# Gathered expert rows through SBUF as whole rows, and four of eight y sums held in PSUM

## What is computed

```
act = gelu(einsum('thkd,td->thk', u[idx], hb))
y   = einsum('thkd,thk->td', v[idx], g * act)      # written here with its operands swapped
x   = x + gate2 * y
```

## Time and profile before

| | |
|---|---|
| median of 3 runs | 3081.89 us (3079.91 to 3082.31) |
| span of the profiled execution | 3916.6 us, 45477 instructions |
| mean granted clock of TensorE in it | 0.894 of 2.4 GHz |
| busy: PE, DVE, POOL, ACT | 3146.4, 2357.3, 1734.0, 1532.9 us |
| first and last gelu of the expert part | 2193.17 and 3870.01 us |

### The profile page before, as it was taken

How to read it: one execution, slowest core, us unless ns; L and a number is a source line. 1 busy time by engine, 2 the same in 40 slices (tenths; PEclk the granted TensorE clock), 3 DMA queues, 4 the chain that set the end, 5 groups by cost and what they waited for, 6 DMA issues and landing times.

```text
span 3916.6 us, 45477 instructions
## 1 busy us (share of the span) xinstructions
PE 3146.4 (80%) x13344; PEld 2447.2 (62%) x13344; DVE 2357.3 (60%) x5010; ACT 1532.9 (39%) x2186; POOL 1734.0 (44%) x1714
## 2 busy tenths in 40 slices
PE   6998899894946749568385888888988998888896
PEld 3787567682735627446264666676766776666765
DVE  4624555451633526446351477787887887877788
ACT  2200543220211202112021356666665666666664
POOL 1002351215245263451523456666665665665663
PEclk8999799996967869678697999999999999999998
DMA  6514412231211212112132577777777777777776
GB/s 214 178 44 175 157 48 76 96 116 47 93 59 57 79 45 91 51 65 88 41 113 81 209 246 255 261 261 266 253 265 253 268 267 255 255 259 256 253 259 236
DMA packets 243601, 645.51 MB, mean 165 GB/s; under 512 B 54688, under 2 KB 55984, under 8 KB 242352
## 3 DMA queue, kind: packets, MB, share of 16 engines
q1 hardware_dynamic: 135856, 371.12, 26.4%
q0 software_dynamic: 107648, 273.25, 20.8%
HBM read 568.46 MB, written 75.76 MB: 164 GB/s over the span
## 4 chain that ended last, share of the span: by engine, by line
PE 30%; issue 17%; DVE 15%; another core or an unknown queue 14%; ACT 4%; DVEq 1%; ACTq 0%; DMA 0%; SPq 0%
PE ra_dots L1548 10%; DVE total L2245 6%; PE ra_dots L1552 5%; PE ex_y L2121 4%; PE ro_q_ps L1746 3%; PE ex_dots L2111 3%; DVE total L2214 2%; ACT ex_vhi L2181 2%; DVE px_ulo L1598 1%; PE ro_q_ps L1751 1%; PE ex_dots L2114 1%; DVE ex_wlo L2202 1%; DVE ex_vlo L2202 1%; ACT ex_prod L2162 1%
## 5 line engine op out<-in xcount | busy, mean ns | idle before, releaser
L2162 ACT ACTIVATE ex_prod<-ex_ring,ex_present 128x512 f32<-128x512 f32 x1024 | 692.6, 685 | 528.3 <-DVE total L2245 389.2
L2081 POOL DMA_INDIRECT ex_ring<-peer_v_dram,sp_row x512 | 534.0, 1043 | 503.7 <-ACT ex_prod L2162 375.1
L1718 POOL DMA_INDIRECT gate_scratch<-ro_dense_gate,ro_dense_place x512 | 502.0, 981 | 448.6 <-DVE ro_dense_gate L1875 293.6
L2245 DVE TENSOR_TENSOR total<-total,ex_prod 128x512 f32<-128x512 f32 x1016 | 670.8, 682 | 22.2 <-issue 13.4
L2076 POOL DMA_INDIRECT ex_pick<-act_scratch,sp_place x512 | 497.8, 972 | 244.2 <-issue 157.4
L1548 PE MATMUL ra_dots<-h_hi_a,px_uhi 128*128 128x512 f32 x1024 | 420.5, 411 | 210.1 <-ACT px_uhi L1530 116.9
L1537 DVE SCALAR_TENSOR_TENSOR px_ulo<-px_uhi,px_u 128x512 fp32r<-128x512 f32 x256 | 170.4, 708 | 606.4 <-ACT px_uhi L1530 493.1
L1560 ACT ACTIVATE ra_act<-ra_dots 128x512 f32<-128x512 f32 x128 | 76.7, 599 | 1007.4 <-remote 532.1
L1548 PE MATMUL ra_dots<-h_lo_a,px_uhi 128*128 128x512 f32 x1024 | 416.1, 406 | 57.0 <-issue 57.0
L2121 PE MATMUL ex_y<-ex_vhi,ex_whi 128*128 128x512 f32 x768 | 322.0, 419 | 160.2 <-DVE total L2214 131.9
L1552 PE MATMUL ra_dots<-h_hi_a,px_ulo 128*128 128x512 f32 x1024 | 285.9, 409 | 162.9 <-issue 143.1
(11 more groups left out here) (293 smaller groups left out, 5492.1 us busy)
## 6 DMA issues: line engine op xcount, KB each, us to landing
px_u<-peer_u_dram SPq DMA_DIRECT2D x256, 512.0 KB
px_v<-peer_v_dram SPq DMA_DIRECT2D x128, 512.0 KB
gate_scratch<-clear_zeros SPq DMA_DIRECT2D x16, 2048.0 KB, 18.7
act_scratch<-ra_act SPq DMA_DIRECT2D x128, 256.0 KB
ex_g<-gate_scratch SPq DMA_DIRECT2D x128, 256.0 KB
w_in_raw<-w_ada_dram SPq DMA_DIRECT2D x64, 256.0 KB, 3.5
w_ada_half<-w_ada_dram SPq DMA_DIRECT2D x4, 2048.0 KB, 13.9
ro_raw<-w_peer_q_dram SPq DMA_DIRECT2D x8, 1024.0 KB, 4.9
```

Of the source, the lines that this page charges most:

```text
L1718: nc.gpsimd.indirect_dma_start(elements, bass.IndirectOffsetOnAxis(ap=places[:, i:i + 1], axis=0), dense_gate[:, t, q:q + 1], None).then_i ...
L2081: nc.gpsimd.indirect_dma_start(ring[:, i], None, rows, bass.IndirectOffsetOnAxis(ap=which[:, RING * s + i:RING * s + i + 1], axis=0)).then ...
L2162: nc.scalar.activation(prod[:, h], ring[:, i, h * HALF:(h + 1) * HALF], ACT.Copy, scale=present[:, b, i:i + 1]).then_inc(prod_ready, 1)
L2245: nc.vector.tensor_tensor(total[:, t, at], total[:, t, at], prod[:, h], ALU.add).then_inc(row_added, 1)
```

## The change

`prod` moves from two PSUM banks of half rows to two SBUF buffers of whole rows. ACT's multiply and DVE's addition of the gathered rows then take 1024 elements at a time, 8 of each in a stage. The two banks go to `held`, so 4 of the 8 y blocks stay in PSUM over all stages, and 4 are added by DVE. In each half stage PE makes one y block, then the two held blocks, then the other y block; the stage orders of ACT and DVE are written anew for the smaller counts.

```diff
-    HELD = NY // 4
+    HELD = NY // 2
     ADDED = NY - HELD
+    HALF_STEP = ADDED // 2
...
+        prod = sb("ex_prod", [P, 2, D])
         dots = ps("ex_dots", [P, 2, TBD])
         held = ps("ex_held", [P, HELD, HALF])
         y = ps("ex_y", [P, 2, HALF])
-        prod = ps("ex_prod", [P, 2, HALF])
...
                         if s + 1 < ST:
-                            pool.wait_ge(prod_ready, 2 * (RING * s + i + 1))
+                            pool.wait_ge(prod_ready, RING * s + i + 1)
                             row(s + 1, i)
...
-                    for n in range(3 * part, 3 * part + 3):
-                        if n == 3 * part + 2:
-                            product(held[:, part], b, part, opens, closes).then_inc(held_ready, 1)
-                            pe.wait_ge(y_added, ADDED * s + n - 1)
-                        elif not opens or n >= 2:
+                    for n in range(HALF_STEP * part, HALF_STEP * part + HALF_STEP):
+                        if n % HALF_STEP:
+                            for m in range(HALF_STEP * part, HALF_STEP * part + HALF_STEP):
+                                product(held[:, m], b, m, opens, closes).then_inc(held_ready, 1)
+                        if not opens or n >= 2:
                             pe.wait_ge(y_added, ADDED * s + n - 1)
                         product(y[:, n % 2], b, HELD + n, True, True).then_inc(y_ready, 1)
...
-                def multiply(s, b, j, first):
-
-                    i, h = j // 2, j % 2
+                def multiply(s, b, i, first):
+
                     act.wait_ge(row_in[i], 16 * s + 16)
                     act.wait_ge(pick_weighted, s + 1)
-                    if not first or j >= 2:
-                        act.wait_ge(row_added, 2 * PER * s + j - 1)
-                    nc.scalar.activation(prod[:, h], ring[:, i, h * HALF:(h + 1) * HALF], ACT.Copy,
+                    if not first or i >= 2:
+                        act.wait_ge(row_added, PER * s + i - 1)
+                    nc.scalar.activation(prod[:, i % 2], ring[:, i], ACT.Copy,
                                          scale=present[:, b, i:i + 1]).then_inc(prod_ready, 1)
...
-                        dve.wait_ge(row_added, 2 * PER * s + j - 2 * NA + 1)
-                        nc.vector.tensor_tensor(total[:, t, at], total[:, t, at], prod[:, h], ALU.add).then_inc(row_added, 1)
+                        dve.wait_ge(row_added, PER * s + i - NA + 1)
+                        nc.vector.tensor_tensor(total[:, t], total[:, t], prod[:, i % 2], ALU.add).then_inc(row_added, 1)
...
                         weigh(s, c)
-                        sums(3 * c)
+                        sums(HALF_STEP * c)
                         rows(c, 0, 1)
                         if not last or n + 2 < CH:
                             low_u(n + 2, c)
                         rows(c, 1, 2)
                         low_weights(s, b, c)
                         rows(c, 2, 3)
-                        sums(3 * c + 1)
-                        rows(c, 3, 5)
-                        sums(3 * c + 2)
-                        rows(c, 5, 8)
+                        sums(HALF_STEP * c + 1)
+                        rows(c, 3, RING // 2)
```

## The result

The changed kernel takes 3193.31 us (3180.63 to 3200.57), beside 3082.1 us (3079.91 to 3082.83) for the kernel before: 1.0358 times as long (1.0343 to 1.0373), 111 us more. 3157 had been predicted, within 3046 to 3225, so direction and range hold, and the loss is one and a half times the predicted 75 us. Ratios and their intervals are of the executions within 1.5% of the fastest of their kernel, which leaves out two of `whole_held2`, given there, and three of `after_one_more`.

The account below looks back on a forecast made before the run. PE was taken to bound the stage at 22.2 us, POOL after the change at 23.4: +1.2 us over 64 stages, +77, and -2 for the ends, on 3081.9 gives 3157 us, within 3046 to 3225.

Parts of the forecast that it names:

- The rule read from the earlier trace: POOL's indirect DMA starting during a DVE instruction with two SBUF operands ends 0.82 us after that instruction.
- POOL's walk: One half stage followed in DVE's new order: eight DMAs in 11.7 us, 23.4 us a stage.
- The even spread: POOL's DMA starts spread evenly over DVE's instructions: 0.20 us lost for each DMA, 24.3 us a stage.
- the stage before: Expert part of the kernel before: 22.2 us a stage, PE's floor of 21.7 and 0.5 for waits on DVE's sums.
- The stage after: Expert part of the changed kernel: bound by POOL at 23.4 us a stage, +1.2 us, over 64 stages +77 us.
- The gain of 32 us: PE's waits on DVE's sums go, 0.5 us in each of 64 stages, if nothing else is late.
- rival A: PE stays the bound and regains its waits: 3048 us, or 3064 with half recovered; chance 0.22 together with D.
- The end: Behind the last stage: DVE has 1.7 us less, `finish` takes 0.1 us more; net -2 us.
- The halts: PE's "remote" waits, 825.1 us in expert part and routing, taken as only in the recorded execution.
- The signs: Expert-part DMA means near 1.20 and 1.12 us, singles to 2.0; POOL's wait for ACT down over 100 us.

Follow-up runs that it names:

- whole_held2: Changed kernel with two y blocks held instead of four, six sums a stage: four executions, 3102.97 to 3175.26 us; ratio 1.0131 of the lower two.
- after_one_more: Changed kernel plus one DVE reduction of 512 zeros in each half stage, on the chip with halts: 3899.06 us, 1.0006 of the kernel before.
- psum_operand: Two held blocks, whole rows in SBUF, but the row addition reads zeros in PSUM instead of `total`: 3078.64 us, 0.9991 of the kernel before.
- after_no_elements_4: Changed kernel without the element gathers behind the first eight: 3079.93 us, 0.9995 of the kernel before.
- half_sbuf: Kernel before with `prod` in SBUF, still as half rows, two y blocks held: 3101.47 us, 1.0070 of the kernel before.
- half_sbuf_held4_5: Changed kernel's four held blocks, but products and additions of half rows in SBUF: 3083.21 us, 1.0005 of the kernel before.
- after_one_more_5: Changed kernel plus one DVE reduction of 512 zeros in each half stage, where the kernel before takes some 3082 us: 3193.23 us, 1.0350.
- before_again: Kernel before, unchanged, profiled once more on the chip of the first experiments: 3080.67 us, span 3078.9.

## Why the prediction was right, and what it missed

- **The mechanism** is shown, each link by a run: whole-row additions with both operands in SBUF lengthen the gathers (`psum_operand` takes that away, and with it all that `whole_held2` loses), POOL's issue becomes the bound (`after_no_elements_4` relieves it in the changed kernel itself, and all 111 us are gone), and half rows in the same place cost 20 us (`half_sbuf`) or nothing (`half_sbuf_held4_5`). The rule read from the earlier trace rows, an end 0.82 us after the instruction, holds for 572 of 574 gathers that start well inside one. It says too little of those that start together with one: most lose nothing, some the whole, and in `after_one_more_5` 11 were held over three or four such instructions in a row.
- **POOL's walk** gave 11.7 us a half stage and 23.4 a stage; 11.65 and 23.3 were measured over all, 23.5 without the opening. So close a hit is in part luck. Two of the walk's eight gathers pass free by nothing: the one at 4.75 starts together with a whole-row addition, the one at 5.99 starts 0.02 us behind its end. In the changed kernel's expert part 93 gathers that start with such an instruction lose nothing and 11 lose up to 1.1 us. The even spread (24.3) was rightly set aside, and `half_sbuf` shows how far off it can be: by even spread I expected 73 us there, and 20 came. The reason, that POOL falls into step with DVE, was in neither estimate by name, but the walk has it in it, since it keeps the order.
- **The term that was mis-sized** is the stage before. "I take 22.2: the floor and 0.5 for waits of PE on DVE's sums" should have been 21.74, what `before_again` takes without the opening. Over the 61.5 stages that remain that is 28 us of the loss. The stage after, 23.53 there, came out 0.13 longer than the walk, 8 us more. The opening has no such loss and gives some 5 back: 31 of the missing 36 us. The 131.9 us of waits in the earlier trace rows are 2.3 us in `before_again`; the rest came with the halts. The gain of 32 us that this allowed the change, in the forecast and in rival A, didn't exist: PE was at its floor already, and where there are no halts, none of the kernels here is more than 3 us faster than the kernel before.
- **The end** was costed at -2 us and is +10.4. I counted DVE's instructions behind the last stage and not what they wait for. POOL is late there too: its last gather ends 22.1 us after the last gelu in the changed kernel (3163.77) and 9.4 us after it in `before_again`. The last products and additions of the changed kernel:

```profile
3162.34 1.43 POOL L2082 DMA_INDIRECT ex_ring<-peer_v_dram,sp_row  x1 [0.30 <-issue]
...
3168.76 1.15 ACT L2162 ACTIVATE ex_prod<-ex_ring,ex_present 128x1024 f32<-128x1024 f32 x1 [1.34 <-DMA ex_ring<-peer_v_dram,sp_row]
...
3171.26 1.15 ACT L2162 ACTIVATE ex_prod<-ex_ring,ex_present 128x1024 f32<-128x1024 f32 x1 [1.35 <-DMA ex_ring<-peer_v_dram,sp_row]
3172.44 1.23 DVE L2244 TENSOR_TENSOR total<-total,ex_prod 128x1024 f32<-128x1024 f32 x1 [1.27 <-ACT ex_prod L2162]
```

The last four rows land 2.5 us apart, though POOL issued them 1.2 to 1.7 us apart. The windows over the end, with columns as above, of the changed kernel:

```profile
3162.00:3167.00 5.00, 5.00 (x18) 4.01 (x17) 2.78 (x3) 1.89 (x2) 1.46 (x2) 0.73 1.01 379
3167.00:3172.00 5.00, 0.54 (x3) 0.12 (x1) 3.05 (x3) 2.31 (x3) 0.00 (x0) 0.95 1.03 419
```

The DMA engines are full there. SP's eight loads of `x1` for `finish`, 512 KB each, which go out as the slots come free, run beside the late rows. In `before_again` the share at the like place is 0.81 to 0.94. Behind its last gather, though, the changed kernel ends after 34.9 us and `before_again` after 37.2, and the five other kernels that keep all gathers after 33.9 to 38.0, if the chip has no halts. So the 12.6 us by which POOL is late cover the 10.4 by themselves. How much of the rest the full DMA engines make up was not tried. The sum of the whole: 31 us for the stages (107.9 less the 76.8 that 64 stages at +1.2 were to cost), 12 for the end and 1.5 ahead of the expert part are 45. Less 7 by which the profiled execution lies above its median and 1.4 by which `before_again` lies below its own, that is the missing 36.
- **The halts.** That the timed executions don't have them was right, and the sum rested on it. "Something that only the recorded execution has" was wrong as to the cause: on one chip all executions have them, so the recorded one most likely ran on such a chip. The span of the changed kernel there, expected within 40 us of 3916.6, wasn't measured; `after_one_more`, the kernel nearest to it, has 3889.8.
- **The signs.** Gathers of rows at 1.16 us for the foretold 1.20 and of elements at 1.18 for 1.12, single ones near 2.0, ACT's wait for rows: all there, though the two groups came out the other way round. PE still waits 79.0 us, for `wlo` and not for sums. ACT's product of 1024 takes 1.15 us, not the 1.05 of a copy, 0.8 us a stage on an engine with room. POOL's wait for ACT fell by 50 us or more against `before_again`. The 100 foretold stood against the 375.1 of the earlier trace rows; without the halts there were only 70.7 to lose.
- **Still open** is why two held blocks lose less than four (3103 to 3175 us against 3181 to 3201), and why the executions with two lie so far apart. The order of DVE decides which gathers meet an addition; which difference in it matters wasn't separated. The pause of 0.30 us between POOL's gathers is in every profile and stays unexplained.

The Trainium skill, page "SBUF — State Buffer", section "SBUF: two separate sides", says that the port shared by VectorE and GpSimd goes to one of them for its whole instruction. The ends 0.82 us behind the addition, however long that is, agree with it. The 4.37 us of one gather, held over four instructions in a row, go beyond one instruction. Its inference that a `tensor_tensor` leaves descriptor generation alone doesn't hold for these gathers, which read their indices in SBUF: 1.98 us against 0.95 with one operand moved.

## What to carry to other kernels

Count the instructions of VectorE that read two SBUF operands wherever GpSimd issues indirect DMAs close to its limit: moving an operand from PSUM to SBUF can cost more than the instructions that it saves, and one instruction of 1.22 us cost more here than two of 0.69, into whose rhythm GpSimd fell. Walk the order by hand rather than spread the events evenly, the end of the pipeline too, and note which steps of the walk turn on a few hundredths of a microsecond. And before costing a gain from a less loaded engine, find out whether the bound has any idle time at all: floor x count was 21.7 us here, and the kernel was at it.

## What the runs showed of the hardware that was not expected

- One chip ran the same kernel in 3883 us and others in 3082, with halts of TensorE of some 5 us laid to "remote", where single elements are gathered or scattered. Without the gathers it took 3605 us. A profile and a median may thus be of chips that differ: compare the span with the median before reading stage times.
- Multiplying 1024 elements from SBUF by a scale for each partition takes ScalarE 1.15 us, a plain copy of as many 1.045.
- A gather that starts together with an addition of two SBUF operands can be held over all such instructions that follow without a break: up to 4.37 us in `after_one_more_5` (11 of 1024), none above 2.03 in the changed kernel.
- VectorE's addition of 1024 with one operand in PSUM takes 1216 ns, with both in SBUF 1228. The operand's place costs VectorE itself nothing.
